# Expert stage: a third pair of PSUM banks in rotation, sums taken out later, the last tile stored in halves, and one GpSimd product placed later

## The reference, cut to what matters

```python
# h: 512 tokens x 1024; per token and head 16 of 16384 experts are chosen
expert = e1 * N_KEYS + e2                    # 8 heads x 16 slots for each token
gate = softmax(top_s)
u = take(peer_u, expert)                     # a row of 1024
a = einsum("cd,chkd->chk", h, u)
w = gate * gelu(a)
vv = take(peer_v, expert)                    # a row of 1024
y = einsum("chk,chkd->cd", w, vv)
x = x + gate2 * y
```

## Time and profile before

| | |
|---|---|
| median of 3 runs | 2904.53 us (2904.18 to 2908.96) |
| the profiled execution | 2909.28 us, span 2907.2 us |
| PE busy | 2427.2 us (83%) |
| DVE busy | 2107.1 us (72%) |
| POOL busy | 1183.1 us (41%) |
| ACT busy | 1005.5 us (35%) |
| gathers (queue q0) | 536.91 MB, 44.7% of 16 engines' span |
| chain that ended last | DMA 20%, PE 13%, DVE 7% |

### The profile page before, as it was taken

How to read it: one execution, slowest core, us unless ns; L and a number is a source line. 1 busy time by engine, 2 the same in 40 slices (tenths; PEclk the granted TensorE clock), 3 DMA queues, 4 the chain that set the end, 5 groups by cost and what they waited for, 6 DMA issues and landing times. The chain is left out here.

```text
span 2907.2 us, 36383 instructions
## 1 busy us (share of the span) xinstructions
PE 2427.2 (83%) x12256; PEld 1686.2 (58%) x12256; DVE 2107.1 (72%) x4034; ACT 1005.5 (35%) x2031; POOL 1183.1 (41%) x972
## 2 busy tenths in 40 slices
PE   7998979999999999999987988866766666766665
PEld 7998979999999896555565433322222222222222
DVE  7466857777777886455555777788878888788876
ACT  3222245666666622344343222222222222221221
POOL 3453446666666430111122434434444444443442
PEclk9999989999999999999998999988888888888899
DMA  3332831222222164101015999999999999999998
GB/s 113 87 95 80 246 92 54 59 58 58 58 58 58 38 195 123 26 27 30 8 51 219 398 418 415 418 394 421 422 421 416 394 421 421 415 390 421 421 421 337
DMA packets 271501, 668.51 MB, mean 230 GB/s; under 512 B 13685, under 2 KB 203290, under 8 KB 205578
## 3 DMA queue, kind: packets, MB, share of 16 engines
q0 software_dynamic: 73952, 536.91, 44.7%
q1 hardware_dynamic: 196816, 129.73, 15.2%
q10 hardware_dynamic: 602, 0.24, 0.0%
HBM read 664.74 MB, written 2.10 MB: 229 GB/s over the span
## 5 line engine op out<-in xcount | busy, mean ns | idle before, releaser
L2468 PE MATMUL peer_py<-peer_uv,peer_diag 128*128 128x512 f32 x1536 | 835.6, 691 | 353.2 <-ACT peer_diag L2382 331.1
L2145 POOL DMA_INDIRECT peer_uv<-k_peer_uv,peer_idx x512 | 504.7, 986 | 776.9 <-PE peer_py L2468 725.4
L2468 PEld LDWEIGHTS peer_py<-peer_uv,peer_diag 128*128 128x128 f32 x1536 | 320.2, 221 | 829.8 <-issue 821.4
L2257 DVE SCALAR_TENSOR_TENSOR peer_spare<-peer_uv,peer_hp 128x1024 bf16<-128x1024 f32 x512 | 622.4, 1217 | 235.5 <-DMA peer_uv<-k_peer_uv,peer_idx 233.8
L1265 PE MATMUL hgrn_pp<-p_hx,p_whl 128*128 128x264 f32 x3024 | 394.1, 288 | 0.7 <-POOL p_whl L1118 0.7
L1265 PEld LDWEIGHTS hgrn_pp<-p_hx,p_whl 128*128 128x128 f32 x3024 | 377.0, 190 | 1.7 <-POOL p_whl L1118 1.1
L2374 ACT ACTIVATE peer_ga<-peer_a 128x2 f32<-128x2 f32 x256 | 52.0, 203 | 844.9 <-DVE peer_spare L2257 843.7
L1118 POOL TENSOR_TENSOR p_whl<-p2n_w,p_whl 128x1024 fp32r<-128x1024 f32 x62 | 147.9, 2396 | 205.3 <-ACT p_whl L1163 205.3
L772 PE MATMUL pool_ps<-p_raw,pool_wh 128*128 128x264 f32 x1024 | 172.0, 291 | 15.6 <-POOL pool_wl L899 10.3
L2382 ACT ACTIVATE peer_diag<-keep_ident,peer_wt 128x128 f32<-128x128 f32 x384 | 140.1, 396 | 115.3 <-DVE peer_wt L2266 112.6
L899 POOL TENSOR_TENSOR pool_wl<-pool_w,pool_wh 128x1024 fp32r<-128x1024 f32 (+1 forms) x48 | 103.0, 2148 | 155.0 <-ACT pool_wh L839 155.0
(11 more groups left out here) (434 smaller groups left out, 4245.7 us busy)
## 6 DMA issues: line engine op xcount, KB each, us to landing
p2n_w<-in_hgrn_w_in SPq DMA_DIRECT2D x62, 512.0 KB
pool_w<-in_pool_w_in SPq DMA_DIRECT2D x32, 512.0 KB
pool_out_aw<-in_w_ada SPq DMA_DIRECT2D x16, 768.0 KB, 4.8
hgrn_out_aw<-in_w_ada SPq DMA_DIRECT2D x16, 768.0 KB, 4.8
p_w<-in_w_pq SPq DMA_DIRECT2D x10, 1024.0 KB
peer_uv<-k_peer_uv,peer_idx POOLq DMA_INDIRECT x512
pool_out_w<-in_pool_w_out SPq DMA_DIRECT2D x7, 1024.0 KB, 7.7
p3a_wf<-in_w_in SPq DMA_DIRECT2D x12, 512.0 KB
```

The source lines that it names most:

```text
L2145: pool.indirect_dma_start(out=uv[:, n % DEPTH].rearrange("p w d -> p (w d)"), out_offset=None, in_=io["k_peer_uv"], in_offset=bass.Indirec ...
L2257: dve.scalar_tensor_tensor(out=spare[:, n % 2, :], in0=uv[:, n % DEPTH, 0, :], scalar=1.0, in1=hp[:, t % 2, :], op0=ALU.mult, op1=ALU.mult ...
L2468: last = pe.matmul(py[:, h * 512:(h + 1) * 512], diag[:, products(n) % DIAGS, :], uv[:, n % DEPTH, 1, h * 512:(h + 1) * 512], start=n % (P ...
```

## The change

- `hp`, `py` and the place of the token transposes, now called `px`, take turns in three pairs of banks, `acc`: in tile t they are pairs 2t, 2t + 1 and 2t + 2 (mod 3). `px` of tile t becomes `hp` of tile t + 1.
- `turn_x` moves from ahead of a tile's first slot to behind slot 8, and waits for the sums of the tile before to be out (`summed`). `take_x` moves on ACT to behind the diagonals of slots 10 and 11. `turn_h` moves from slot 8 to slot 13 in the tiles behind the first.
- `store` becomes three: `add_sums` at slot 2 of the next tile, `gate_rows` at slot 14, `add_tokens` at slot 15.
- The last tile is finished in two halves of 512 columns, each stored by itself, and a semaphore `half_used` tells DVE that the first half of `py` is complete.
- POOL's product `chosen(s + 1)` moves from behind the fetch of slot 6 to behind that of slot 9.

```diff
+        acc = ph.ps("acc", [P, 3, D])
+        hp = [acc[:, 2 * t % 3, :] for t in range(TT)]
+        py = [acc[:, (2 * t + 1) % 3, :] for t in range(TT)]
+        px = [acc[:, (2 * t + 2) % 3, :] for t in range(TT)]
...
-            for t in range(TT):
+            for t in range(TT - 1):
                 sp.wait_ge(y_taken, t + 1)
                 sp.dma_start(out[0, t * P:(t + 1) * P, :], rows[:, t % 2, :]).then_inc(stored[t % 2], 16)
+            t = TT - 1
+            for h, cols in enumerate(HALVES):
+                sp.wait_ge(y_taken, t + 1 + h)
+                sp.dma_start(out[0, t * P:(t + 1) * P, cols], rows[:, t % 2, cols]).then_inc(stored[t % 2], 16)
...
                     gather(s, k)
-                    if k == 6 and s + 1 < UNITS:
+                    if k == 9 and s + 1 < UNITS:
                         chosen(s + 1)
...
-            def store(t):
+            def add_sums(t):
                 dve.wait_ge(v_used, products((t + 1) * PH * TOPK))
                 dve.wait_ge(v_added, (t + 1) * PH * TOPK // SHARE)
                 if t >= 2:
                     dve.wait_ge(stored[t % 2], 16 * (t // 2))
+                dve.tensor_tensor(rows[:, t % 2, :], py[t], running[:, :], ALU.add).then_inc(summed, 1)
+
+            def gate_rows(t):
+                dve.wait_ge(summed, t + 1)
+                dve.tensor_tensor(rows[:, t % 2, :], rows[:, t % 2, :], g2[:, :], ALU.mult).then_inc(scaled, 1)
...
+            def last_store():
+                t = TT - 1
+                dve.wait_ge(v_added, UNITS * TOPK // SHARE)
+                dve.wait_ge(stored[t % 2], 16 * (t // 2))
+                dve.wait_ge(x_taken, t + 2)
+                for h, cols in enumerate(HALVES):
+                    if h == 0:
+                        dve.wait_ge(half_used, 1)
+                    else:
+                        dve.wait_ge(v_used, products(UNITS * TOPK))
+                    dve.tensor_tensor(rows[:, t % 2, cols], py[t][:, cols], running[:, cols], ALU.add).then_inc(summed, 1)
...
-                    if k == 1 and s % PH == 0 and s:
-                        store(s // PH - 1)
+                    if s % PH == 0 and s:
+                        if k == 2:
+                            add_sums(s // PH - 1)
+                        if k == 14:
+                            gate_rows(s // PH - 1)
+                        if k == 15:
+                            add_tokens(s // PH - 1)
...
             for s in range(UNITS):
                 t = s // PH
-                if s and s % PH == 0:
-                    pe.wait_ge(y_taken, t)
-                    turn_x(t)
-                    pe.wait_ge(x_taken, t + 2)
...
-                    if s % PH == 0 and k == 8 and t + 1 < TT:
-                        pe.wait_ge(dotted, t * PH * TOPK)
+                    if s and s % PH == 0 and k == 8:
+                        pe.wait_ge(summed, t)
+                        turn_x(t)
+                    if s % PH == 0 and k == (13 if s else 8) and t + 1 < TT:
+                        pe.wait_ge(x_taken, t + 2)
                         turn_h(t + 1)
```

More of the change, by code:

```diff
@@ L2058, in peer_phase @@
     AHEAD = 2
+    HALVES = (slice(0, D // 2), slice(D // 2, D))
     with Phase(nc, "peer") as ph:
@@ L2359, in _ @@
             act.wait_ge(x_turned, 1)
-            act.activation(g2[:, :], py[:, :], ACT.Copy).then_inc(x_taken, 1)
+            act.activation(g2[:, :], px[0], ACT.Copy).then_inc(x_taken, 1)
             take_q(1, None, FIRST)
@@ L2383, in _ @@
                            .then_inc(diag_done, 1)
+                    if s and s % PH == 0 and at == 5:
+                        take_x(s // PH)
                     if s == 0 and at in (0, 1):
@@ L2467, in _ @@
                         for h in range(2):
-                            last = pe.matmul(py[:, h * 512:(h + 1) * 512], diag[:, products(n) % DIAGS, :],
+                            last = pe.matmul(py[t][:, h * 512:(h + 1) * 512], diag[:, products(n) % DIAGS, :],
                                              uv[:, n % DEPTH, 1, h * 512:(h + 1) * 512], start=n % (PH * TOPK) == 0,
                                              stop=n % (PH * TOPK) == PH * TOPK - 2)
+                            if n == UNITS * TOPK - 2 and h == 0:
+                                last.then_inc(half_used, 1)
                         last.then_inc(v_used, 1)
```

40 lines of the change are left out of this document (19 added, 21 removed).

## The result

| | before | changed |
|---|---|---|
| median | 2907.71 us (2904.18 to 2909.22, 5 runs) | 2933.29 us (2929.41 to 2942.09, 5 runs) |
| profiled execution (span) | 2909.28 us (2907.2) | 2935.15 us (2932.8) |

The ratio is 1.0094, interval 1.0075 to 1.0114. The prediction was 2910.0, range 2897 to 2919.

A forecast was written before the change was run, and what follows sets the result against it. In the expert stage the DMA fetches were taken as the bound, with the dots as the measure. The terms -2.5 + 1.2 - 1.2 + 8 gave +5.5 us: 2914.8 on the profiled execution, 2910.0 on the median, range 2897 to 2919.

The forecast's parts named there:

- Rival C: Tile boundaries: bytes are the measure and the holes are paid in full, -13.5 us, 2890 to 2895; chance 0.13.
- uneven DMA engines: Tile boundaries: one of 16 DMA engines runs later than the rest and catches up in a hole; no size of its own.
- (1): Tile boundaries: three rotating pairs of banks remove POOL's 10.24 us wait, worth 2.5 us by the dots.
- (2): Sums leaving at slots 2, 14 and 15 of the next tile: 0.4 us a tile, +1.2 us.
- (3): Last tile in halves: earlier sums and a smaller last store gain 0.5 to 1.5 us, taken as 1.2.
- (4): Index product behind slot 9's fetch: DVE's reduction waits for it, costing the first tile 0 to 19 us, taken as 8.
- 0 to 19: First tile's loss by the index wait: units 1 to 4 give 6 to 15, units 5 and 6 0 to 2 each.
- Units 7 to 31 lose nothing: Units 7 to 31: a 4.5 us delay by the index wait fits narrowly within 5.4 us of slack, costing 0.
- The slack of 5.4 us: Unit 10, fetch of slot 12: used 11.5 us after issue, against 6.1 us with an empty queue.
- rival D: Later tiles: the index wait starves them too, 20 us on top of the first tile's loss, 2920 to 2930; chance 0.12.
- A: First tile: the index wait costs more than the boundaries give back, +0 to +10, 2905 to 2915; chance 0.52.
- The 6.1 us: Fetch of slot 2 in unit 1: shortest time from issue to use, with an empty queue, used to reckon slack.

The follow-up runs named there:

- e1: Changed kernel with POOL's index product back behind the fetch of slot 6 instead of slot 9; ratio 1.0009 to the kernel before.
- e14: e1 measured again, in more rounds; ratio 0.9999 to the kernel before.
- e8: Kernel before with 16 idle POOL products ahead of slot 8's fetch in units 12, 20 and 28, a hole; ratio 1.0043.
- e3: Changed kernel, product still behind slot 9, with DVE's reduction and indices at slots 6 and 7 instead of 3 and 4; ratio 0.9999 to before.
- e5: Changed kernel with the index product behind the fetch of slot 8 instead of slot 9; ratio 0.9999 to the kernel before.
- e7: Changed kernel with the product behind slot 6 and PE's projections in units 1 to 6 cut from 8 chunks to 1; ratio 1.0005 to before.
- e12: Changed kernel with the product behind slot 6 and all three sums at slot 2 instead of 2, 14 and 15; ratio 0.9981 to before.
- e13: e12 measured again, in more rounds; ratio 1.0003 to the kernel before.
- e15: Kernel before with its last tile finished and stored in two halves, nothing else; ratio 1.0003 to the kernel before.
- e9: The changed kernel itself, measured again; ratio 1.0087 to the kernel before.
- e2: Kernel before with the index product behind the fetch of slot 9, nothing else; 2951.06 us, ratio 1.0158 to the kernel before.
- e4: Changed kernel with the product behind slot 9 in the later tiles only, slot 6 in the first tile; ratio 1.0029 to before.

## Why the prediction was wrong

**The bound and the measure: right.** The stage runs at the rate of the gathers, and the dots, not the bytes, tell what a hole costs. Rival C, 13.5 us for the boundaries, is out: e1 and e14 have no such holes (from 1925 to 1955 e1 has 421 GB/s, before had 354) and no gain. That a hole is given back in part rests on e8. That uneven DMA engines are the reason is only argued; no row here shows the single engines. What fits is that a quiet unit of 40.73 us at 421 GB/s moves 17.1 MB, though its 16 fetches have 16.8: the bytes run ahead of the dots. The Trainium skill (DMA: Bandwidth & Descriptors, "Why a DMA increments its semaphore by 16 and not by 1") says that the engines finish independently, not that one is slower.

**(1) The rotation, -2.5: some 1.6 in the traces, not seen in the time.** The dots of slot 10 in units 7, 9, 15, 17, 23 and 25 of the changed kernel, beside the earlier trace rows:

```profile
1931.54 1.21 DVE L2264 SCALAR_TENSOR_TENSOR peer_spare<-peer_uv,peer_acc 128x1024 bf16<-128x1024 f32 x1
...
2012.95 1.21 DVE L2264 SCALAR_TENSOR_TENSOR peer_spare<-peer_uv,peer_acc 128x1024 bf16<-128x1024 f32 x1
...
2259.71 1.21 DVE L2264 SCALAR_TENSOR_TENSOR peer_spare<-peer_uv,peer_acc 128x1024 bf16<-128x1024 f32 x1
...
2341.43 1.22 DVE L2264 SCALAR_TENSOR_TENSOR peer_spare<-peer_uv,peer_acc 128x1024 bf16<-128x1024 f32 x1 [0.21 <-issue]
...
2587.13 1.21 DVE L2264 SCALAR_TENSOR_TENSOR peer_spare<-peer_uv,peer_acc 128x1024 bf16<-128x1024 f32 x1
...
2668.38 1.22 DVE L2264 SCALAR_TENSOR_TENSOR peer_spare<-peer_uv,peer_acc 128x1024 bf16<-128x1024 f32 x1
```

The boundary pairs take 81.41, 81.72 and 81.25 us, 5.5 less than before in all, and the rate at the first is 390 GB/s instead of 318. But the six quiet units between, 243.68 before, now take 246.76. What the rotation gives at the boundary, the wait at slot 3 takes back behind it. Without that wait the rotated kernel's three pairs take 246.8 to 248.5 us in seven executions (e1, e3, e5, e7, e12, e13, e14), and the old order's 248.0 to 250.3 in three (before, e8, e15). That is 1.6 us between the means, and the ranges touch. The medians are level with before within 0.1%, in which 1.6 us isn't seen. The term was small, as forecast, and somewhat too large.

**(2) and (3): small, as said.** The late sums had +1.2: e13 against e14 says nothing within 0.1%. The halves had -1.2: 0.9 by the trace. One estimate was off. I took half of 1.23 us for an addition of half width. It takes 0.69, as these rows of the changed kernel's end show (the first addition of each half).

```profile
2926.09 0.69 DVE L2317 TENSOR_TENSOR peer_rows<-peer_acc,peer_running 128x512 f32<-128x512 f32 x1 [0.58 <-PE peer_acc L2496]
...
2928.15 0.68 DVE L2317 TENSOR_TENSOR peer_rows<-peer_acc,peer_running 128x512 f32<-128x512 f32 x1
```

**(4) The index product, +8: this step failed.** Its mechanism was right. In the first tile it cost 24.7 us (22.9 in e9) and not 8. The price that the rows gave for a unit, 3.7 us with the cold start, was near the 4.5 measured in units 1 to 4, but in part by luck, since two of its terms were off in opposite ways:

| term, us a unit | forecast | measured, mean of units 1 to 4 |
|---|---|---|
| reduction later | 3.5 (4.5 in unit 2) | 2.5 (2.3 in unit 2) |
| slack at the next unit's first fetch | -2.0 | -0.45 |
| cold start at slot 2 | 2.2 | 2.5 |
| sum | 3.7 | 4.5 |

What failed was the choice within 0 to 19: "I take 8 ... since part of the cold start is moved and not added". PE's start at slot 0 became a little warmer in unit 2 (5.37 us for two products instead of 6.12), and that is in the 2.3 already. But it still idles 4.37 us there and starts cold, and it starts cold once more at slot 2, in each of units 1 to 6 at the full price of 3.75 us instead of 1.96. The rows gave no size for the moving; they gave 3.7 a unit, and the upper end of 15 to 19 was the reading. The second failure is the extent: units 5 and 6, put at 0 to 2, lose 1.3 and 4.5, so that the first tile loses 24.7 and not at most 19. They lose 1.0 and 3.1 in e9 but nothing in e2 (-0.4 and 0.3), so why they lose in the rotated kernel stays open.

**"Units 7 to 31 lose nothing": wrong by some 8 us** (e4: 0.29%). The slack of 5.4 us from the earlier trace rows was that of one fetch in one unit, but it wasn't used up either: in units 8 to 30 the fetch of slot 12 is used 11.3 us after its issue before, on average, and 8.6 in the changed kernel. PE starts slot 2's product wholly or partly cold in these units too, 2.6 to 3.75 us. The mean rate of the quiet stretch fell from 419 to 410 GB/s. Where in a unit the third of a microsecond is lost isn't shown. This is rival D's case at two fifths of its size. D had asked for a delay of 6.7 and 20 us.

**So:** the time is A's mechanism at more than the upper end of its price, and a part of D, 0.9% where the sum said 0.2%. Both add on the same side, and the range, cut at 2919, counted the two as alternatives. A and D aren't rivals: the same wait feeds both.

The 6.1 us of the earlier trace rows from issue to use wasn't the floor that I called it. With the queue drained by the late fetches, (2,12) of the changed kernel took from 1699.20 to 1704.84, 5.6 us. The Trainium skill's figure for a transfer (DMA: Bandwidth & Descriptors, "Anatomy of one DMA — SWDGE (gpsimd) path") gave 5.3 us by my estimate, and this fetch comes near it.
